# Regrouping the eviction of the pool mixer's results and the first weight split inside the attention units

## What is computed

```python
d = jnp.stack(outs, axis=2)                       # (S, 4 groups, 128): window mean minus token
y_pool = (jnp.einsum('bsgc,gcd->bsgd', d, pool_w).reshape(B, S, 512) * pool_scale) @ w_pool_out

for i in range(8):                                # 8 blocks of 128 queries, 8 heads, keys up to the block's end
    s = einsum('bhqd,bhkd->bhqk', q_block, k) * 64 ** -0.5 + c_q - c_k
    s = where(mask, s, -1e30)
    out = einsum('bhqk,bhkd->bhqd', softmax(s), v)

x = x + (g_pool * y_pool + g_fox * (out @ w_fox_out)) @ w_out
```

## Time and profile before

| | |
|---|---|
| time, median of 3 executions | 1436.48 (1435.26 to 1436.6) |
| the profiled execution's own time | 1435.91 |
| span of its trace | 1434.0 |
| PE busy | 1410.4 (98%) |
| DVE busy | 1005.1 (70%) |
| ACT busy | 644.1 (45%) |
| POOL busy | 562.8 (39%) |
| granted clock of TensorE, mean | 0.999 |

### The profile page before, as it was taken

One profiled execution on the slowest core, in us unless ns is written; L12 is line 12 of the kernel. 1 busy time (PEld: TensorE's weight loads), 2 busy tenths in 40 slices (PEclk: granted clock), 3 DMA queues, 4 the chain that ended last, 5 costly groups with the idle time before them and its releaser, 6 DMA issues.

```text
span 1434.0 us, 19452 instructions
## 1 busy us (share of the span) xinstructions
PE 1410.4 (98%) x7017; PEld 1163.3 (81%) x7017; DVE 1005.1 (70%) x1457; ACT 644.1 (45%) x1215; POOL 562.8 (39%) x574
## 2 busy tenths in 40 slices
PE   8999999999899999999999999999999999999998
PEld 5878888887688888888888788888888888888886
DVE  7846495646877637877657887777767777795867
ACT  6545343435877653546443532333323322444445
POOL 5833243334545412023012654454444443354402
PEclk9999999999999999999999999999999999999999
DMA  8164264546332298314203113333323335883334
GB/s 214 50 129 118 55 136 100 74 83 212 111 118 90 74 283 193 111 50 131 65 7 133 60 62 107 110 111 110 110 83 109 110 111 199 304 283 99 92 103 147
DMA packets 108105, 173.71 MB, mean 121 GB/s; under 512 B 7485, under 2 KB 63313, under 8 KB 106474
## 3 DMA queue, kind: packets, MB, share of 16 engines
q1 hardware_dynamic: 99016, 148.18, 35.2%
q0 software_dynamic: 5408, 15.76, 4.2%
q10 hardware_dynamic: 3586, 8.52, 1.6%
HBM read 125.42 MB, written 42.30 MB: 117 GB/s over the span
## 4 chain that ended last, share of the span: by engine, by line
PE 88%; POOL 4%; DVE 3%; ACT 3%; issue 1%; DMA 1%; DVEq 0%; SPq 0%; ACTq 0%; POOLq 0%
PE ps L2313 27%; PE ps L2315 27%; PE ps L2314 27%; PE ps L2498 2%; PE ps L2507 1%; PE ps L2536 1%; ACT prob L1325 1%; PE ps L2537 1%; POOL w_lo L875 1%; PE ps L2366 1%; DMA w_raw<-in_w_xkv 1%; DVE prob L1896 1%; PE ps L2673 0%; PE ps L2320 0%; DMA x_t<-in_x 0%
## 5 line engine op out<-in xcount | busy, mean ns | idle before, releaser
L2313 PE MATMUL ps<-t_lo,s_hi 128*128 128x512 f32 x308 | 119.9, 389 | 0.1
L2314 PE MATMUL ps<-t_hi,s_hi 128*128 128x512 f32 x308 | 119.8, 389 | 0.0
L2315 PE MATMUL ps<-t_hi,s_lo 128*128 128x512 f32 x308 | 119.8, 389 | 0.0
L2313 PE MATMUL ps<-h_lo_T,w_hi 128*128 128x512 f32 x256 | 100.5, 393 | 1.3 <-ACT u_t L1236 1.0
L1534 ACT ACTIVATE s_hi<-w_raw 128x512 fp32r<-128x512 f32 x77 | 48.7, 632 | 118.0 <-PE ps L2315 91.7
L1619 DVE TENSOR_TENSOR s_lo<-w_raw,s_hi 128x512 fp32r<-128x512 f32 x77 | 62.2, 808 | 56.1 <-ACT s_hi L1534 55.9
L2315 PE MATMUL ps<-h_hi_T,w_lo 128*128 128x512 f32 x256 | 99.7, 389 | 0.0
L2314 PE MATMUL ps<-h_hi_T,w_hi 128*128 128x512 f32 x256 | 99.6, 389 | 0.0
L1550 ACT ACTIVATE p_sb<-ps 128x512 f32<-128x512 f32 x22 | 13.0, 598 | 187.3 <-PE ps L2315 177.0
L2313 PE MATMUL ps<-hf_lo_T,w_hi 128*128 128x512 f32 x212 | 82.5, 389 | 0.0
L2314 PE MATMUL ps<-hf_hi_T,w_hi 128*128 128x512 f32 x212 | 82.5, 389 | 0.0
(11 more groups left out here) (399 smaller groups left out, 4373.7 us busy)
## 6 DMA issues: line engine op xcount, KB each, us to landing
w_raw<-hs_dram SPq DMA_DIRECT2D x77, 256.0 KB, 2.7
raw_p<-in_w_ffn_in SPq DMA_DIRECT2D x22, 512.0 KB, 4.6
w_raw<-in_w_ffn_in SPq DMA_DIRECT2D x22, 512.0 KB, 4.2
hs_dram<-h_sum SPq DMA_DIRECT2D x11, 1024.0 KB, 9.0
hs_dram<-hq SPq DMA_DIRECT2D x11, 768.0 KB, 7.1
wq_B<-in_w_ffn_out SPq DMA_DIRECT2D x8, 1024.0 KB, 7.6
raw_f<-in_w_in SPq DMA_DIRECT2D x14, 512.0 KB, 7.3
gate_dram<-c_st SPq DMA_DIRECT2D x28, 256.0 KB, 2.2
```

Of the source, the lines that this page charges most:

```text
L2313: nc.tensor.matmul(dst, w_h, x_l, start=start, stop=False, skip_group_check=onto)
L2314: nc.tensor.matmul(dst, w_h, x_h, start=False, stop=False, skip_group_check=onto)
L2315: return nc.tensor.matmul(dst, w_l, x_h, start=False, stop=stop, skip_group_check=onto)
```

## The change

Three tables get other values; no instruction is added or removed.

```diff
-SPLIT_AT = {5: 0, 7: 1, 12: 2, 18: 3, 23: 4, 28: 5, 32: 6}
-LOW_AFTER = {5: 0, 8: 1, 12: 2, 18: 3, 24: 4, 28: 5}
+SPLIT_AT = {3: 0, 7: 1, 12: 2, 18: 3, 23: 4, 28: 5, 32: 6}
+LOW_AFTER = {3: 0, 8: 1, 12: 2, 18: 3, 24: 4, 28: 5}
-MIXED_IN = {8: (0, 1), 9: (2, 3), 10: (4, 5, 6), 11: (7,)}
+MIXED_IN = {8: (0, 1), 9: (2, 3), 10: (4, 5), 11: (6, 7)}
```

## The result

The change makes the kernel slightly slower: 1438.23 median of 18 executions (1436.34 to 1442.81) against 1436.21 of before in 18 executions beside them (1435.26 to 1437.08). The ratio is 1.0017, with a 95% interval of 1.001 to 1.0023. The range of the prediction, 1435.1 to 1438.8, holds, and so does its call that the time stays within 0.2%, but neither by much, and its 1437.4 is 0.8 too low: 0.95 more than before was forecast, 2.0 more is measured. What stands out is the spread: nine executions lie at 1436.3 to 1437.8, nine at 1438.6 to 1442.8. The profiled execution, 1439.73 with a span of 1437.8, is one of the upper nine.

A forecast was written before the change was run, and what follows sets the result against it. The prediction took PE, busy for 1410.4 of 1434.0, to bound the kernel. A loss of 1.6 less a gain of 0.65 is 0.95, added to 1436.48 for 1437.4; range 1435.1 to 1438.8.

The forecast's parts named there:

- What bounds: Whole kernel: PE busy 1410.4 of 1434.0, so only its few microseconds of waits in the touched units can change.
- The lock between DVE and POOL: Unit 4: POOL's moved split blocks DVE's q part, costing 0.7 at PE's transposes; DVE's later k parts run unblocked.
- POOL's masks: Unit 5: masks behind the moved split, plain blocks back about 357.0, DVE wanting them about 357.4; cost 0 to 0.5.
- part 1: Chunk 0 split in unit 3 instead of 5: scores of unit 8 start 0.9 sooner, 0.25 goes again, 0.65 gained.
- Part 2: Result 6 in unit 11: head 1's scores in unit 12 wait for DVE's low part to free bank 3; 1.6 lost.
- The sum: Whole kernel: 1.6 lost less 0.65 gained is 0.95, giving a median of 1437.4; forecast chance 0.60.
- The clock: Rival, unit 12: PE's waits drop the granted clock to 0.50, adding 3.3, time 1440.7; chance 0.04.
- the case that I called likeliest: Whole kernel: both the loss and the gain arise and the clock stays up, 1437.4; chance 0.60.

The follow-up runs named there:

- masks_first: Kernel before with only chunk 0's split moved earlier, its low part on POOL put behind the masks for unit 5: 1435.36 beside 1436.26, ratio 0.9993.
- busy_wait: The whole change plus eight thrown-away matmuls in PE's wait between head 0's and head 1's scores in unit 12: 1437.2 beside 1435.9, ratio 1.001.
- whole_again: The whole change, unaltered, measured once more against the kernel before: 1438.08 beside 1436.26, ratio 1.0012.
- mixed_only: Kernel before with only result 6 moved to unit 11, chunk 0 still split in unit 5: 1438.83 beside 1435.9, ratio 1.0023.
- mixed_again: The same kernel as mixed_only, measured once more against the kernel before: 1440.58 beside 1436.08.
- fill_first: The whole change plus three thrown-away matmuls in PE's first wait of unit 12, the second left idle: 1437.86 beside 1436.08.

## Why the prediction was right, point by point

**What bounds.** Right. Only the waits of PE in units 5 to 12 moved, and the later stages kept their times.

**The lock between DVE and POOL.** Right in kind: the q part was blocked to 355.05 (353.52 + 1.53), 0.6 behind POOL's end at 354.5, and the k parts ran free. Its cost was less than the 0.7 at PE: the scaling of unit 4 ended only about 0.2 later, because DVE reached the q part sooner (353.52 against 353.79 in the earlier trace rows; 0.22 of it remains when both are counted from the transposes of unit 0) and the scaling ran a little faster. In both stretches POOL now did no masks beside DVE. masks_first, in which it does them there again, bears this out: DVE reaches the q part 13.86 after the transposes of unit 0, just as before.

**POOL's masks: "just in time, cost 0 to 0.5".** This is the term that failed. I took nothing of it into the sum, and it was the dearest thing in part 1: DVE's bias of unit 5 waited 0.56, and masks_first shows that this order cost about 0.5 at unit 12. Both sides of "just in time" were off. DVE was ready at 356.98 and not at 357.4. POOL's set of four masks took 2.6 (354.45 to 357.07) and not 2.0, and the two put-backs behind them another 0.5, so the plain blocks were back at 357.53 and not at 357.0. With the masks first part 1 brings 0.95; as it was, 0.42 and not the 0.65 of the sum. The start of the scores of unit 8 was forecast at 371.5 and came at 371.42, but then 0.54 and not 0.25 was given back to ACT's copies.

**Part 2.** Right in place and order, and nearly in size: the wait ahead of head 0's scores is 0.66 shorter, head 1's wait "over 2" stands between them (2.09), released by the low part on DVE. Forecast 1.6, measured 1.42 with the clock up.

**The sum.** 0.95 forecast, 1.00 in the distance of busy_wait, 1.1 in time between the lower nine executions (median 1437.35) and before (1436.21). That these agree so well is luck: two errors of 0.2 cancelled. It is luck as well that the median stayed in the range. All this holds where the clock stays up; the other half of the executions has a median of 1440.06, outside the range, and with one or two more of them in this half the median of all would have left the range too. The measured rise of the median, 2.0, is twice the forecast.

**The clock.** Here it was the chance that was wrong, more than the price. I gave it 0.04, on the ground that a wait of 1.42 had left the clock alone. In the profiled execution it fell with 0.76 idle, 0.65 of scores and 2.09 idle, and by their times in about half of the others. The price, 3.3 forecast, was 2.5 in the profiled execution. So the median isn't the case that I called likeliest, but a mixture of two, and lies 0.8 above it. The rival at least gave the upper half a name; its time, 1440.7, lay outside the range. The Trainium skill's warning ("TensorE: Matmul & The Clock Gate", section "HAM oscillation — how this bites in real kernels") deserved more weight than one trace that hadn't shown a fall: it tells of a clock that fell in the pauses between bursts of matmuls, and that trace had no idle time of this size between its matmuls once they were under way (the longest waits there are 1.5). Here a pause of 2.09 agrees with it.

## What to carry to other kernels

When a result is moved one step later, ask which bank or buffer it holds, who writes there next, and behind what on the evicting engine it now stands: here one 0.7 instruction behind the scaling instead of ahead of the bias made a wait of 2.1. On this kernel, in which TensorE is 98% busy, the idle time added in unit 12 (0.76 and 2.09 instead of 1.42) cost its length, 1.4, and in part of the executions the clock as well; look at the granted clock by stretches and at the spread, not only at the median or at the mean clock. Cost a split that moves to another engine's list by everything that it pushes back there, not only by what it blocks while it runs.

## What the runs showed of the hardware

- TensorE's granted clock fell from 1.00 to 0.50 during a wait of 2.09 that followed one of 0.76 and 0.65 of work, and came back at about 399. From the stretches (0.62 and 0.67 in two of 2.0 are 1.5 and 1.3 at the low level, and 4.0 between them) it was low for 6.8; whole_again and mixed_only give 6.8 too, mixed_again 3.4. Eight thrown-away matmuls in the wait, 2.04 long, kept it at 1.00. It also stayed at 1.00 through one wait of 2.13 (fill_first), and fell behind one of 2.15 in another stage (mixed_again).
- Judged by their times, the fall doesn't come in every execution of the same program: in roughly half of those of the changed kernel, in eight of nine of mixed_again.
- A DVE instruction with two SBUF inputs that meets a POOL tensor-tensor of 2.4 stands until that ends and then takes 0.5 to 0.6 more (1.53 instead of 0.68 for the one, 3.42 instead of 1.41 for the pair), while the bias instruction, with one input in the accumulator, ran beside it at its usual 0.82.
